# Reordering the first mixer of a two-block decoder kernel: RWKV branch first, compact decay levels, 64-column chunk matrices, inverse roots on ScalarE

## What is computed

```python
p = u @ w_in                      # 1024 -> pool 256 | HGRN 4*256 | RWKV 1024 | GLA 4*256 + 16
y_pool = causal_multiscale_pool(p_pool, ...)
# HGRN and GLA: chunked gated linear attention, 4 heads of 64
#   scores[t,s] = sum_k q[t,k] k[s,k] exp(b[t,k] - b[s,k]) for s <= t;  o = scores @ v
y_hgrn = rms_norm(o_h, hgrn_norm) * sigmoid(hg)
y_gla  = o_g * rsqrt(mean(o_g^2) + eps) * gla_norm * silu(gg)
# RWKV-7, per head, S is 64 x 64
#   p_rw = p_rw + (prev_token - p_rw) * mu;  decay = exp(-exp(w_log));  a = sigmoid(...)
#   kk = kk / max(sqrt(sum kk^2), 1e-12);  rk = rk * (1 + (a - 1) * k_a)
#   S_t = S_{t-1} diag(w_t) - (S_{t-1} kk_t)(kk_t a_t)^T + v_t k_t^T;  o_t = S_t r_t
y_rwkv = (group_norm(o_r) * ln_w + ln_b + bonus) * g_r
x = x + concat(y_pool, y_hgrn, y_rwkv, y_gla) @ w_out
```

## Time and profile before

| | |
|---|---|
| runs shown | 1722.61 us median of 3 (1722.0 to 1726.46) |
| the profiled execution, its own time | 1723.34 us |
| its span | 1721.5 us, so 1.8 us lie around it |
| TensorE busy in the span | 94% |
| granted TensorE clock, mean | 0.968 of full |
| one 512 KB weight block, issue to landing | 3.7 us (median of 419) |

### The profile page before, as it was taken

One profiled execution on the slowest core, in us unless ns is written; L12 is line 12 of the kernel. 1 busy time (PEld: TensorE's weight loads), 2 busy tenths in 40 slices (PEclk: granted clock), 3 DMA queues, 4 the chain that ended last, 5 costly groups with the idle time before them and its releaser, 6 DMA issues.

```text
span 1721.5 us, 23078 instructions
## 1 busy us (share of the span) xinstructions
PE 1622.0 (94%) x8902; PEld 1384.5 (80%) x8902; DVE 1080.1 (63%) x1431; ACT 702.8 (41%) x1029; POOL 850.1 (49%) x992
## 2 busy tenths in 40 slices
PE   6999999958899999899999999999999997699998
PEld 5888888737688888788888788887688886578887
DVE  5866455976358666876645596643576646448664
ACT  5544421020055545544515455442455432345542
POOL 5966300200069667776600396640686630059664
PEclk9999999958799999999999999999999999899999
DMA  6665533200146555465534456553565542046553
GB/s 242 209 184 172 159 134 110 87 1 1 37 159 206 190 172 191 141 208 187 187 125 156 147 197 190 183 189 123 173 204 190 172 143 98 13 158 209 185 183 110
DMA packets 107197, 263.56 MB, mean 153 GB/s; under 512 B 9168, under 2 KB 43088, under 8 KB 106960
## 3 DMA queue, kind: packets, MB, share of 16 engines
q1 hardware_dynamic: 107088, 262.09, 46.5%
HBM read 261.00 MB, written 1.05 MB: 152 GB/s over the span
## 4 chain that ended last, share of the span: by engine, by line
PE 86%; DVE 11%; ACT 1%; issue 1%; DMA 1%; SPq 0%; DVEq 0%; ACTq 0%
PE ps L1396 37%; PE ps L1397 21%; PE ps L1427 11%; PE ps L1473 4%; PE ps L1399 4%; PE ps L1484 2%; DVE xn L796 1%; DMA raw<-blocks 1%; DVE arena L1349 1%; PE ps L1777 1%; PE ps L1548 1%; DVE arena L1001 1%; DVE arena L1301 1%; PE ps L1443 1%; PE ps L1707 1%
## 5 line engine op out<-in xcount | busy, mean ns | idle before, releaser
L476 POOL TENSOR_TENSOR w_lo<-raw,w_hi 128x256 fp32r<-128x256 f32 x976 | 837.9, 892 | 724.6 <-ACT w_hi L530 721.1
L1396 PE MATMUL ps<-xn,w_hi 128*128 128x512 f32 x1848 | 666.7, 399 | 25.2 <-DVE xn L796 22.7
L1397 PE MATMUL ps<-xn,w_lo 128*128 128x256 f32 x2112 | 553.3, 282 | 0.0
L530 ACT ACTIVATE w_hi<-raw 128x1024 fp32r<-128x1024 f32 (+1 forms) x468 | 426.3, 920 | 200.3 <-PE ps L1399 109.6
L1396 PEld LDWEIGHTS ps<-xn,w_hi 128*128 128x128 f32 x1848 | 349.5, 189 | 104.7 <-DVE xn L796 14.6
L1397 PEld LDWEIGHTS ps<-xn,w_lo 128*128 128x128 f32 x2112 | 401.4, 190 | 17.9 <-DVE xn L796 0.4
L1396 PE MATMUL ps<-hid,w_hi 128*128 128x512 f32 x1008 | 364.0, 397 | 2.0 <-DVE w_lo L789 2.0
L1397 PE MATMUL ps<-hid,w_lo 128*128 128x256 f32 x1056 | 292.8, 282 | 0.0
L789 DVE TENSOR_TENSOR w_lo<-raw,w_hi 128x512 fp32r<-128x512 f32 (+1 forms) x218 | 248.0, 1138 | 36.7 <-ACT w_hi L530 31.8
L1396 PEld LDWEIGHTS ps<-hid,w_hi 128*128 128x128 f32 x1008 | 190.3, 189 | 43.5 <-issue 2.3
L866 DVE TENSOR_TENSOR arena<-ps,low_part 128x512 f32<-128x512 f32 x132 | 90.8, 688 | 205.7 <-ACT low_part L591 205.6
(11 more groups left out here) (281 smaller groups left out, 1151.8 us busy)
## 6 DMA issues: line engine op xcount, KB each, us to landing
raw<-blocks SPq DMA_DIRECT2D x419, 512.0 KB, 3.7
raw<-blocks SPq DMA_DIRECT2D x144, 256.0 KB, 3.5
cst<-consts SPq DMA_DIRECT2D x1, 2358.0 KB, 14.4
x<-x_in SPq DMA_DIRECT2D x4, 256.0 KB, 5.8
out<-x SPq DMA_DIRECT2D x4, 256.0 KB, 3.3
cst<-consts SPq DMA_DIRECT2D x1, 109.0 KB, 2.1
```

The lines of the kernel that those rows point to most:

```text
L476: ins = nc.gpsimd.tensor_tensor(w_lo[:, slot(n), piece], raw[:, slot(n), piece], w_hi[:, slot(n), piece], ALU.subtract)
L530: nc.scalar.activation(w_hi[:, slot(n), cols], raw[:, slot(n), cols], ACT.Copy)\
L1396: nc.tensor.matmul(where, hi, both.rearrange("p a t -> p (a t)"), start=opens, stop=False)
L1397: ins = nc.tensor.matmul(where[:, 0:SEQ], lo, high, start=False, stop=False)
```

## The change

Tile order: the 27 input tiles now come as RWKV's eight, GLA's nine, the pool's two, HGRN's eight. Two tiles (instead of four) run while the norm is being computed, and from the ninth tile on they alternate between PSUM banks 6 and 7 alone. Output rows start as soon as pool and GLA are ready, and go between RWKV's states and HGRN's levels. SyncE issues the same blocks in the new order.

```diff
+MIX_IN_ORDER = (25, 26, 21, 22, 19, 20, 23, 24) + tuple(range(9)) + (17, 18) + tuple(range(9, 17))
+MIX_BANKS = (6, 7, 0, 1, 6, 7, 0, 1) + (6, 7) * 10
+MIX_OUT_ORDER = ((4, 6), (5, 7), (0, 0), (1, 1), (6, 4), (7, 5), (2, 2), (3, 3))
```

Decay levels: level 0 becomes one product q*k, summed over each head by a matmul (`own_token`). Levels 1 to 8 multiply only the half of the columns that the level uses:

```diff
-                    chain(tt(q_dec[b][:, :, :], src["q"][:, :, :], decay_to[:, :, :], ALU.mult))
-                    signal(tt(k_dec[b][:, :, :], src["k"][:, :, :], decay_from[:, :, :], ALU.mult), "gla_qk")
+                ins = tt(q_dec[b].rearrange("p (m s) -> p m s", s=n), by_level(flat(src["q"]), n, 1), by_level(to, n, 1), ALU.mult)
+                if n > 1:
+                    ins = tt(by_level(flat(k_dec[b]), n, 0), by_level(flat(src["k"]), n, 0), by_level(frm, n, 0), ALU.mult)
+                signal(ins, "gla_qk")
...
-                    signal(nc.vector.copy_predicated(scores[:, :, :], mask, pair(b)), "sc_out")
+                for j in range(2):
+                    out = scores[k - 1][:, 4 * j:4 * j + 4, :].rearrange("p a (m e s) -> p a m e s", e=2, s=n)[:, :, :, 1, :]
+                    ins = nc.vector.copy_predicated(out, mask, ps[:, b + j, 0:SEQ].rearrange("p (a m s) -> p a m s", a=4, s=n))
...
-                            ins = mm(ps[:, b + j, (2 * c + t) * P:(2 * c + t + 1) * P], k_of[rows, c, cols],
-                                     q_of[rows, c, cols], start=True, stop=True)
+                            ins = mm(ps[:, b + j, m * CHUNK:(m + 1) * CHUNK], k_of[rows, c, t * P:t * P + P], q_of[rows, c, t, :],
+                                     start=True, stop=True)
```

Chunk matrices: each product of two 64-token chunks is a matmul of its own with 64 rows of contraction, 64 weight columns and 64 moving columns. Sixteen of them make a group; they replace eight 128x128 matmuls:

```diff
+                def products(b, lhs, rhs):
+                    for c, head, t, own, m, cols, tok in heads_and_chunks():
+                        ins = mm(ps[own, b + m // 4, (m % 4) * CHUNK:(m % 4 + 1) * CHUNK], lhs[head, c, tok], rhs[head, c, tok], start=True, stop=True)
+                def chunk_products(b, lhs, rhs):
+                    for c, head, t, own, m, cols, tok in heads_and_chunks():
+                        ins = mm(bank(b, 8)[own, m, :], lhs[own, m, :], rhs[own, m, :], start=True, stop=True)
+                def inverse_y(lev):
+                    need(pe, "rw_z_out", lev)
+                    chunk_products(3, l_t, inv).then_inc(ev["rw_y"], 1)
+                def inverse_z(lev):
+                    need(pe, "rw_ym", lev)
+                    if lev < 5:
+                        chunk_products(4, inv_t, y_m)
+                    chunk_products(5, y_m, inv_t).then_inc(ev["rw_z"], 1)
```

TensorE's stream weaves them in. In GLA's part:

```diff
+                for lev in range(2, 9):
+                    tile()
+                    if lev % 2:
+                        inverse_y((lev + 3) // 2)
+                    else:
+                        inverse_z(lev // 2 + 1)
                     attention_level(lev, gla_in, 1)
```

Roots: where a square root on ScalarE was followed by a reciprocal on VectorE, ScalarE now does both, and the reciprocal of the decays becomes an exponential (the scan now adds up rates, and `cum` and `inv_cum` are both exponentials of the sum). Copies of PSUM results (a_tok, b_tok, k_tok, v_tok, lv, w_t, u, v_rows, the far scores, o_r) move from VectorE to ScalarE:

```diff
+                def inverse_root(out_ap, src, features, eps, name):
+                    chain(nc.scalar.activation(out_ap, src, ACT.Ln, scale=1.0 / features, bias=eps))
+                    nc.scalar.activation(out_ap, out_ap, ACT.Exp, scale=-0.5).then_inc(ev[name], 1)
...
-                chain(nc.vector.reciprocal(sq[:, :, :], sq[:, :, :]))
-                chain(nc.vector.reciprocal(by_chunk(inv_cum), after))
-                chain(nc.vector.reciprocal(rms_r[:, :, :], rms_r[:, :, :]))
```

More of the change, by code:

```diff
@@ L370, in build @@
[L370 to L382, removed]
+        ga_sb = h
@@ L608, in in_place @@
                     nc.scalar.activation(ap, ap, func).then_inc(ev["fn_done"], 1)
[L610 to L614, removed]
-                need(act, "gla_abs", 1)
-                chain(nc.scalar.activation(tmp2[:, :, :], tmp2[:, :, :], ACT.Exp, scale=-1.0))
@@ L1013, in inverse_norm @@
-            def inverse_norm(k, c):
-                need(v, "on_root", k)
-                chain(nc.vector.reciprocal(norm_sb[:, c, :], norm_sb[:, c, :]))
+                chain(tt(o_sb[:, :, :], bank(2 if k == 1 else 7), o_diag[:, :, :], ALU.add))
+                signal(tt(o_sq[:, :, :], o_sb[:, :, :], o_sb[:, :, :], ALU.mult), "o_sq")
             def normalise(per_head):
@@ new lines, in mixer_one @@
+                signal(tt(sq[:, :, :], kk[:, :, :], kk[:, :, :], ALU.mult), "rw_kk_sq")
+                mix_tile(4)
+                need(v, "rw_rate", 1)
+                need(v, "folds", 1)
+                signal(nc.vector.tensor_tensor_scan(flat(total_rate), flat(go_on), flat(rate), 0.0, ALU.mult, ALU.add), "rw_scan")
+                mix_tile(5)
+                chain(shifted(0))
+                need(v, "rw_kk_n", 1)
+                signal(tsc(sq[:, :, :], bank(2), 1e-24, None, ALU.max), "rw_kk_max")
@@ new lines, in mixer_one @@
+                need(v, "rw_iclr", 1)
+                for c in range(2):
+                    ins = tsc(k_new[:, c, :], iclr[:, c, :], -1.0, const("k_a", c), ALU.add, ALU.mult)
+                chain(ins)
+                chain(stt(k_new[:, :, :], k_new[:, :, :], 1.0, k_in, ALU.add, ALU.mult))
+                mix_tile(6)
+                need(v, "rw_kk_rn", 1)
+                chain(tt(kk[:, :, :], kk[:, :, :], sq[:, :, :], ALU.mult))
+                after, before = cum[:, :, 1:], cum[:, :, 0:CHUNK]
@@ new lines, in mixer_one @@
+                tile()
+                need(pe, "rw_mat_out", 3)
+                products(4, kk_dec, r_dec)
+                need(pe, "rw_tok_out", 4)
+                for c, head, t, own, m, cols, tok in heads_and_chunks():
+                    ins = mm(bank(3)[own, t, cols], lak_t[own, m, :], v_tok[own, t, cols], start=True, stop=True)
+                ins.then_inc(ev["rw_lv"], 1)
+                tile()
+                need(pe, "rw_bonus_in", 1)
+                need(pe, "rw_lv_out", 1)
+                mm(ps[:, 3, :], const("head_ones"), flat(sq), start=True, stop=True).then_inc(ev["rw_bonus"], 1)
@@ new lines, in mixer_one @@
+                new_state(3)
+                attention_level(4, hgrn_in, 2)
+                rows(1)
+                of_state(3)
+                attention_level(5, hgrn_in, 2)
+                need(pe, "rw_u_out", 3)
+                for c, head, t, own, m, cols, tok in heads_and_chunks():
+                    q = tok.start // CHUNK
+                    o = bank(4)[head, c, tok]
+                    if q:
+                        mm(o, state[q][head, c, :], r_dec[head, c, tok], start=True, stop=False)
+                    mm(o, u[:, t, cols], mrb_t[:, m, own], start=q == 0, stop=False)
+                    ins = mm(o, v_tok[:, t, cols], mrk_t[:, m, own], start=False, stop=True)
@@ L1761, in lru @@
+                rows(4, 5, 6, 7)
+                taken[0] += 27
             def lru():
```

933 lines of the change are left out of this document (526 added, 407 removed).

## The result

| | before | after |
|---|---|---|
| runs, median (us) | 1723.09 of 4 (1722.0 to 1726.46) | 1651.36 of 4 (1649.76 to 1652.52) |
| span of the profiled execution (us) | 1721.5 | 1649.6 |
| mixer's first and last matmul (us) | 206.9, 487.3 | 206.8, 416.0 |
| next FFN's first matmul (us) | 489.5 | 418.2 |

The ratio of the times is 0.9583, with a 95% interval of 0.9569 to 0.9598. By the medians 71.7 us were saved where 75.7 were forecast; 1651.4 stands against 1648.0, inside the range. By the spans it is 71.9, and 71.2 of them lie between the mixer's first and last matmul. The rest of the kernel gave 0.7.

What follows compares the result with a forecast made beforehand. TensorE bounds the kernel, so gains come from its idle time, slow clock and work. Start 15.2 + 23.5, middle 110.7, tail 53.9, GpSimd 1.4 = 204.7 us against 280.4, 75.7 less: 1648 from 1723.3, range 1630 to 1676.

Steps and rivals of the forecast that it cites:

- What bounds the mixer: Mixer's 280.4 us of matmuls: 38 us TensorE idle, 27 slow clock, about 215 work; RWKV is a chain between TensorE and VectorE.
- Start: From 206.9 us through the first two product groups: 15.2 plus 23.5 us, with five tiles hiding the kk chain.
- Middle: 18 tiles with levels, inverse steps and product groups between them: 110.7 us, TensorE leading VectorE in GLA's part.
- Tail: Behind the last tile: 35 us of TensorE work, 5.1 of waits with handshakes, then rows 4 to 7; 53.9 us.
- output product 2.8: Term of the tail's TensorE work: RWKV's output product takes 2.8 us.
- Roots: Norm roots: three 3.35 us reciprocals leave VectorE; ScalarE's ln 0.69, load 1.28, exp 0.63 make 2.6 us on the path.
- Transfers, and after the mixer: Same 35 blocks, covered by six slots filled ahead; the next FFN waits for the last rows as before: nothing charged.
- One bank serializes: Rival: chunk products of y, z, lv, u in one PSUM bank run one after another, 12.8 us more: 1661; 20%.
- Four tiles at once: Rival: four 64x64 tiles of the array really run at once, 10 us less: 1638; 12%.
- VectorE bounds the tail and the clock falls: Rival: tail paced by VectorE, clock 0.6, TensorE's 35 us of small work loses 14: 1662, or 1665 with GpSimd; 14%.
- Each small matmul paid whole: Rival: changing array quarter drains the array, about 420 small matmuls paid at latency; at 0.5 us each 1828; 3%.
- The freed time does not come back: Rival: first tiles stall on RWKV's start or a load, new gaps meet every saving: 1718 to 1723; 1%.

## Why the prediction was right, step by step

**What bounds the mixer.** Right. TensorE idle and slow behind a chain with VectorE was the largest part, and 55 of the 71 us came from there. The unwoven inverse (16.0 us) and the late rows (13.8) show two pieces of it separately. The RWKV-first order as a whole, the reordered blocks and GpSimd's tables were not undone by themselves, so what they bring is argued and not shown.

**Start.** The first two product groups end at 244.1; forecast with the 1.4 for GpSimd was 247.0. GpSimd's tables cost nothing visible (TensorE 35.62 of 36 us busy beside them), and the two groups took 1.14 instead of 2.3.

**Middle.** From there to the last tile's end 107.5 us against 110.7. Turns of 7.2 and 6.3 against 7.3 and 6.4: tile, level, y and z were priced within 0.15 us each, and VectorE, with 21.5 of 34 us, no longer sets the pace. The difference is three product groups and w at 0.67 instead of 1.15, and the levels at 1.53 instead of 1.64.

**Tail.** 64.4 us against 53.9, and here is the error. The step that failed is the term "output product 2.8": it measured 8.0. I had priced its 44 matmuls by rows in which column halves alternate, and had not looked at the order of the shapes in the new stream, though the diff shows it. Of the 5.2 us too little, 3.6 are the changes of shape and 1.5 the missing alternation (1.32 in the 32 products with 128 rows, 0.17 in the states). The other term is the clock: I had it at 1.00 through the tail, and a fall between rows 0 and 3 was among my own signs of being wrong. It fell there, and rows 0 and 1 and one level cost 5.26 + 5.34 - 2 x 3.65 + 2.85 - 1.53 = 4.6 us more at 0.50. Waits were about as listed: 0.9, 0.9, 1.1 and 1.6 here for 1.3, 1.3, 1.7 and handshakes there. So start and middle came out 6.1 us early, the tail 10.5 late, together 4.4: row 7 ended at 416.0 for 411.6. That the total came so near is in part luck, two errors against each other.

**Roots.** Right on the path: 0.69, 1.28 and 0.63 as forecast. The loads stand both between logarithm and exponential and behind them, 1.28 us each. The return of four reciprocals (three of 512 columns, one of 256) costs 4.4 us; that of the decays stayed away, and its worth was not tried.

**Transfers, and after the mixer.** Nothing in either, as forecast: no wait on a block is among TensorE's between 205 and 416 us, and from row 7's end to the next FFN it is 2.2 us before and after. But what comes last there is not row 7. In both kernels the chain of waits leaves TensorE 3.4 us before that row's end, through a block's load (3.42 us) and ScalarE's split of it (1.06). So the term was right at nothing because the path is the same before and after.

**The rivals.** *One bank serializes*: false. y, z, lv and u write both row halves into one bank and take 1.08 for sixteen, or 2.01 for 32, not 1.7 each. The twelve state products of the output say the same: in one bank, 1.01 us mostly one behind another in one quarter, 0.84 with the halves alternating. All these lie in different partitions of the bank; two row halves that write the same partitions of one bank were not tried. *Four tiles at once*: true where the matmuls use all four quarters, the products and w (1.14 for two groups, 0.57 each); y and z use only the two quarters on the diagonal and stay at about 1.0. So it brought 3 us, not the 10 of the rival. No run shows those 10, which the lower end of the range uses too: they were my estimate, with the 0.94 halved in all 22 groups. *VectorE bounds the tail and the clock falls*: it happened for two stretches and cost 4.6 of the 14 us it was given. With the rows late it cost 18.4, so the argument against it, that rows in between hold the clock, was right in the main; the kernel with the state work earlier lost 11.3 us to the clock with its rows in between. *Each small matmul paid whole*: false inside a group of one shape, where sixteen take 1.08 us, 0.07 each. A change of shape costs 0.16 us, and the 24 of the output product are the one place where that was measured. *The freed time does not come back*: false.

## What to carry to other kernels

Price a run of small matmuls by its order and not by its count: with the same matmuls, a neighbour in another half of the array took a level from 1.53 to 1.04 us and an output product from 3.34 to 2.02, and sorting by shape took 3.6 us off. A chain between two engines can cost twice, as idle time and as half clock in what follows: with the inverse in one piece it was 9.7 us more idle and 9.0 of clock. So put full-size work between its links even where it fills no gap (without the rows there, 13.9 us more went to the clock and 1.3 to idle time), and then read the clock in short slices: with such work in place it still fell in one order of the matmuls (11.3 us lost) and held at 1.00 in another, and these runs don't show why. And measure a small change at the end of its own stage, since the code behind this mixer, the same in every kernel, took 1227.6 to 1231.6 us.

## What was unexpected of the hardware

- A change between 128*64 and 64*64 matmuls cost 0.16 us each, and nothing else in the record marks it: the matmuls are listed as busy.
- The moving columns of a level hardly count: with the same 128 weight columns and 64 rows, 32 moving columns took 1.48 us for eight matmuls and 64 took 1.53.
- The granted clock was 0.50 for 20 us in which TensorE is recorded as busy without a gap (374 to 394 in the run with the state work earlier), so a full busy column does not vouch for the clock. And waits of the same length before the same two levels (1.16 and 0.63 us, 1.17 and 0.64) were followed by half clock in one order of the matmuls and by full clock in another.
- Two VectorE operations of 1.45 us together were once recorded as 5.62. GpSimd was busy beside them both times, so its being busy is not the whole cause.
